# A decoder step on one core: the second half's stage input by four channel tiles, and feed-forward blocks of 6, 8 and 8 tiles

## Chip, cores and metric

One core of a Trainium2 chip runs the whole program. The metric is the device time of one execution in microseconds (us).

## The reference

A decoder trunk of four layers works on 512 prompt tokens and 64 sample tokens of width 1024. Each layer has a token mixer (gMLP, convolution, MLA, gMLP again) and a feed-forward, each followed by a residual layer norm, and each fed through a scale and shift computed from a condition (adaLN):

```python
for i in range(DEPTH):
    sh1p, sc1p, g1p, sh2p, sc2p, g2p = adaln(c_prompt, ada_w[i], ada_b[i])
    hp = xp * (1 + sc1p) + sh1p
    # op = mixer (i mod 3) of hp; the same for the samples with their own condition
    xp = layer_norm(ALPHA * xp + g1p * op, ln_mix_g[i], ln_mix_b[i])
    fp = swiglu_ffn(xp * (1 + sc2p) + sh2p, ffn_w_gate[i], ffn_w_up[i], ffn_w_down[i])
    xp = layer_norm(ALPHA * xp + g2p * fp, ln_ffn_g[i], ln_ffn_b[i])

def swiglu_ffn(h, wg, wu, wd):
    return (jax.nn.silu(h @ wg) * (h @ wu)) @ wd
```

The feed-forward is 2816 wide. The mixers, their caches and states are computed as well.

## The kernel before

**Layout.** The residual `xa` is kept transposed: 128 channels of each of `KT` = 8 channel tiles on the partitions, 576 tokens (512 of the prompt, then 64 of the samples) along the free axis. Tokens are worked in two halves `h` of `HALF` = 288; half 1 holds the last 224 prompt tokens (`HP`) and all samples.

**Products.** Each fp32 product is made of three fp32r matmuls, high x high, high x low, low x high (L736). The stage input is therefore the pair `h_hi`, `h_lo`, an inner activation the pair `a_hi`, `a_lo`, a weight the pair `w_hi`, `w_lo`. Weights come in units of up to 1024 words per partition through five slots: SyncE loads a unit into `w_raw` (L560) once the product that used the slot's former unit has ended (`plan.freed`, counted in `acc_ready`), GpSimd splits it (L669, L671), and TensorE takes it (`take_units`). The queue of units is laid down in order by `Plan`, and the `plan_` functions repeat the order of the products. Accumulators are four PSUM banks taken in turn (`acc_ready`, `acc_free`); four more banks serve statistics, transposes and adaLN.

**Feed-forward.** Its 22 inner tiles go in three blocks listed in `GU` (L372): gate and up products of a block (`gate_up`), then `down` of that block into all 8 output tiles, added to `xa` by VectorE. The last block's down product is `down_norm`, which also prepares the layer norm. Products that share a block's inner tiles run over as many k tiles as the block has. AdaLN matmuls of the next layer (`ada_pairs`) stand between: four behind the first half of the first two tiles, one behind every tile below 20 (`ada_behind`), one behind each of the first two `down`. For them SyncE puts loads of 1 MB between those of the units.

**Tail of a stage** (`down_norm`, on TensorE, VectorE and ScalarE). TensorE makes output tiles 0 to 3, both halves, then 4 to 7 of half 0, then matmuls against a matrix of ones that sum half 0 (mean and square) in the middle of tile 4 of half 1, then the rest of half 1. VectorE adds each product to `xa` (`add_norm`), reduces sums of tiles and of their squares (`sums` L1705, `squares` L1710), finishes the statistics (`Stats` L1723 to L1729), and normalises `xa` in steps of tiles 0-1, 2-3 and 4-7 (`normalise`, L1734 and L1736), each step counted in `n_ready`. For half 1 it does the same after the first half's input is out.

**Handover to the next stage.** ScalarE (`apply`, L1340) makes `hf` (fp32) and `h_hi` of four tiles at a time from normalised `xa`, two instructions a tile. VectorE then subtracts them into `h_lo` (`halves`, L1762) and counts `h_ready`, four times a stage: half 0 tiles 0-3, half 0 tiles 4-7, half 1 tiles 0-3, half 1 tiles 4-7. For half 1 VectorE first makes the samples' columns of `hf` with their own coefficients (`samples`, L1750), in one go for eight tiles. TensorE's `first_four` makes the first four products of half 0 by halves of k: k 0-3 of all four after the first count, k 4-7 after the second; the statistics of half 1 (`second_stats`) stand after the first of the four is done. These four are `first_halves` (gate and up of two tiles, or the convolution's) or `first_tokens` (two token tiles of two column blocks, for gMLP and MLA). Their results are taken off before half 1's `h_lo`: ScalarE and VectorE call `early()` (`ffn_first`, `conv_first`, `mla_first`, `gmlp_first`). The products of half 1 with the same weights then run one after the other, each over all of k.

The order of every engine is the order of this code; each engine waits for counted semaphores.

Of the kernel before, what the change touches and what calls it, by code (L numbers as in the profile page):

```python
# [97 lines left out]
def trunk(nc, A, O):  # L98
    ctx = ExitStack()
    with ctx:  # L100
# [271 lines left out]
        GU = ((0, 8), (8, 8), (16, 6))  # L372
# [351 lines left out]
        def _(pe):  # L724
# [49 lines left out]
            def product(out, ks, w_at, m_hi, m_lo, w_moves=False, waits=None):  # L774

                n = len(ks)
                for q, k in enumerate(ks):
                    if waits is not None and k % 4 == 0:
                        pe.wait_ge(h_ready, waits + k // 4)
# [90 lines left out]
            def first_halves(t, slots):  # L870

                def step(i, k, b):
                    s, c = slots[i], slice(k * P, (k + 1) * P)
                    for e, (w, a) in enumerate(((w_hi, h_hi), (w_hi, h_lo), (w_lo, h_hi))):
                        last = mm(pb[:, b, 0:HALF], w[:, s, c], a[:, k, 0:HALF], k == 0 and e == 0,
                                  k == KT - 1 and e == 2)
                    return last

                first_four(t, step, lambda _: slots.extend(take_units(2)))  # L880

            def first_tokens(t, slots, widths):

                def step(i, k, b):
                    blk, tt = divmod(i, 2)
                    n = widths[blk]
                    s, c = slots[blk][k // 4], slice(k % 4 * n, (k % 4 + 1) * n)
                    for e, (w, a) in enumerate(((w_hi, h_hi), (w_hi, h_lo), (w_lo, h_hi))):
                        last = mm(pb[:, b, 0:n], a[:, k, token_tile(tt)], w[:, s, c], k == 0 and e == 0,  # L890
                                  k == KT - 1 and e == 2)
                    return last

                def units(blk):
                    slots[blk] = take_units(2)

                first_four(t, step, units)
# [57 lines left out]
            def gate_up(first, count, wait_h, fresh, more):  # L955

                if fresh:
                    slots = []
                    first_halves(wait_h, slots)
                    ada_pairs(ADA_FIRST * more)  # L960
                    for s in slots:
                        half_product(s, KT, 1, (h_hi, h_lo), wait_h)
                for m in range(2 * fresh, count):
                    s_a, s_b = take_units(2)
                    for h in range(2):
                        for s in (s_a, s_b):
                            half_product(s, KT, h, (h_hi, h_lo))
                    ada_pairs(more * ada_behind(first + m))
# [15 lines left out]
            def gmlp(l):  # L984
# [3 lines left out]
                first_tokens(t, slots, (256, 256))  # L988
                for n, (gg, tt) in enumerate(first_order(GROUPS)):
                    if n < 4:  # L990
                        continue
                    if gg not in slots:
# [5 lines left out]
                            w_moves=True, waits=4 * t + 3 if n == 4 else None).then_inc(acc_ready, 1)  # L998
# [36 lines left out]
            def conv(l):  # L1035
# [9 lines left out]
                first_halves(t, slots)  # L1045
                for s in slots:
                    half_product(s, KT, 1, (h_hi, h_lo), t)
# [25 lines left out]
            def tok_major(chunk, tt, kts, hi, lo, waits=None):  # L1073
# [6 lines left out]
                        w_moves=True, waits=waits).then_inc(acc_ready, 1)  # L1080
                G.up()

            def mla(l):
                t = 2 * l
                slots = {}
                first_tokens(t, slots, (DCH[0][1], DCH[1][1]))
                for i, (c, tt) in enumerate(first_order(len(DCH))):
                    if i < 4:
# [3 lines left out]
                    tok_major((slots[c], lambda k: (k // 4, k % 4), DCH[c][1]), tt, KT, h_hi, h_lo,  # L1092
                              4 * t + 3 if i == 4 else None)
# [195 lines left out]
        def _(act):  # L1289
# [32 lines left out]
            def apply(t, early, loads=None):  # L1322

                for h in range(2):
# [5 lines left out]
                    for g in range(2):  # L1331
# [26 lines left out]
            def final():  # L1358
                t = 2 * DEPTH
                for h in range(2):  # L1360
                    deviation(t, h)
                    for m in range(KT):
                        if m in (0, 2, 4):
                            act.wait_ge(n_ready, 6 * t + 3 * h + m // 2 + 1)
# [212 lines left out]
        def _(dve):  # L1577
# [163 lines left out]
            def samples(t):  # L1741
# [3 lines left out]
                if t == 0:  # L1745
                    dve.wait_ge(h_ready, 2)
                o = hf[:, :, :, HP:].rearrange("p g i (b t) -> p (g i) b t", b=DEC_B)
                x = xa[:, :, SEQ:TOK].rearrange("p m (b t) -> p m b t", b=DEC_B)
                for src, coef, op in ((x, cs, ALU.mult), (o, cb, ALU.add)):
                    v.tensor_tensor(o, src, coef[:, t % RING_T, :, 1:NC].unsqueeze(3)  # L1750
                                    .to_broadcast([P, KT, DEC_B, DEC_T]), op)
# [13 lines left out]
            def down_norm(e, early=None, turn=False, by_half=False):  # L1765
# [525 lines left out]
            dve.drain().then_inc(n_ready, 6)  # L2291
            for g in range(2):
                halves(0, g)
            samples(0)
            for g in range(2):
                halves(1, g)
# [74 lines left out]
```

## Time and profile before

| | |
|---|---|
| time, median of 3 | 3607.05 us (3606.09 to 3609.25) |
| profiled execution | 3606.18 us, its span 3604.4 us |
| TensorE (PE) busy | 3241.4 us, 90% |
| VectorE (DVE) busy | 1775.0 us, 49% |
| GpSimd (POOL) busy | 1498.8 us, 42% |
| ScalarE (ACT) busy | 483.0 us, 13% |
| mean granted TensorE clock | 0.947 |

The page gives busy time by engine, then chains of work and costly groups. The timeline lists instructions with their start, duration in us, engine, line, operands, and in brackets the idle time before them with what ended it. A matmul's duration includes its way through the array, so two neighbours overlap; what counts is the distance of their starts. PEclk 1.00 is full clock, 0.50 half. SPq is SyncE's queue that issues loads.

### The profile page before, as it was taken

The page shows a single profiled execution, that of the slowest core. Times are in us where ns is not written, and L with a number is a line of the kernel's source. Part 1 is how long each engine was busy: PE and PEld are TensorE (multiplying, and loading weights), DVE is VectorE, ACT ScalarE, POOL GpSimd, SP SyncE. Part 2 cuts the span into 40 slices and gives each one's busy share as a digit, 9 for nine tenths or more (in the row PEclk, how much of TensorE's full clock was granted, in tenths as well). Part 3 has the DMA queues.
Part 4 walks back from the last instruction along what each step waited for, and adds up shares of the span by engine and source line. Part 5 has one row for each costly group of instructions (what it writes and reads, how often), then busy time and mean ns, then how long its engine had stood idle before and what let it go on. Part 6 is the DMA issues. An engine that isn't in the chain of part 4 may idle for free.

```text
span 3604.4 us, 54522 instructions
## 1 busy us (share of the span) xinstructions
PE 3241.4 (90%) x22732; PEld 2976.4 (83%) x22732; DVE 1775.0 (49%) x2754; ACT 483.0 (13%) x1004; POOL 1498.8 (42%) x876
## 2 busy tenths in 40 slices
PE   5979799999788699999778989999998988899996
PEld 4879789999766489999775548999988987899996
DVE  3174664433677764333654446434253456643436
ACT  2100030000210130000301202100013100210001
POOL 2343445454366445454320013455543343355551
PEclk8999999999899899999987989999998998999998
DMA  5532343442211143442212113534321232132221
GB/s 200 211 87 59 100 159 123 146 129 71 75 52 36 38 166 126 144 129 71 69 34 81 41 42 106 176 120 138 100 77 54 66 89 63 53 92 81 81 83 49
DMA packets 450515, 343.83 MB, mean 95 GB/s; under 512 B 24937, under 2 KB 435937, under 8 KB 437966
## 3 DMA queue, kind: packets, MB, share of 16 engines
q1 hardware_dynamic: 443104, 333.59, 29.3%
q10 hardware_dynamic: 7165, 6.76, 0.7%
q8 instruction: 180, 2.95, 0.3%
q14 instruction: 66, 0.53, 0.0%
HBM read 335.77 MB, written 5.25 MB: 95 GB/s over the span
## 4 chain that ended last, share of the span: by engine, by line
PE 74%; DVE 17%; issue 4%; DVEq 3%; ACT 1%; POOL 1%; POOLq 0%; DMA 0%; ACTq 0%; SPq 0%
PE pb L736 73%; DVE a_lo L1593 1%; DVE xa L1736 1%; DVE pb L2029 1%; DVE a_hi L1591 1%; DVE vn L1939 1%; DVE part L1710 1%; DVEq L1735 1%; DVE pb L1729 1%; DVE h_lo L1762 1%; DVE vn L1935 1%; DVE part L1705 1%; POOL w_lo L671 1%; PE pb L812 1%; DVE pgT L2229 1%
## 5 line engine op out<-in xcount | busy, mean ns | idle before, releaser
L669 POOL TENSOR_SCALAR w_hi<-w_raw 128x1024 fp32r<-128x1024 f32 (+2 forms) x416 | 449.9, 1082 | 1905.4 <-DMA w_raw<-in_ffn_w_up 437.8
L736 PE MATMUL pb<-h_hi,w_hi 128*128 128x288 f32 x3584 | 1084.3, 303 | 71.7 <-DVE h_lo L1762 50.8
L736 PE MATMUL pb<-h_lo,w_hi 128*128 128x288 f32 x3584 | 1071.3, 299 | 0.0
L736 PE MATMUL pb<-h_hi,w_lo 128*128 128x288 f32 x3584 | 1070.6, 299 | 0.0
L671 POOL TENSOR_TENSOR w_lo<-w_raw,w_hi 128x1024 fp32r<-128x1024 f32 (+2 forms) x416 | 964.5, 2319 | 62.4 <-issue 1.7
L736 PEld LDWEIGHTS pb<-h_hi,w_hi 128*128 128x128 f32 x3584 | 689.1, 192 | 123.2 <-issue 101.9
L736 PEld LDWEIGHTS pb<-h_lo,w_hi 128*128 128x128 f32 x3584 | 688.8, 192 | 0.3
L736 PEld LDWEIGHTS pb<-h_hi,w_lo 128*128 128x128 f32 x3584 | 687.8, 192 | 0.0
L736 PE MATMUL pb<-a_hi,w_hi 128*128 128x288 f32 x2176 | 648.3, 298 | 33.4 <-DVEq L2066 11.7
L736 PE MATMUL pb<-a_hi,w_lo 128*128 128x288 f32 x2176 | 642.5, 295 | 0.0
L736 PE MATMUL pb<-a_lo,w_hi 128*128 128x288 f32 x2176 | 642.2, 295 | 0.0
L736 PEld LDWEIGHTS pb<-a_hi,w_hi 128*128 128x128 f32 x2176 | 409.7, 188 | 43.7 <-issue 30.4
L736 PEld LDWEIGHTS pb<-a_lo,w_hi 128*128 128x128 f32 x2176 | 409.5, 188 | 0.9
L736 PEld LDWEIGHTS pb<-a_hi,w_lo 128*128 128x128 f32 x2176 | 409.6, 188 | 0.0
L1854 DVE TENSOR_TENSOR pr<-pb,sg 128x288 f32<-128x288 f32 x176 | 80.2, 458 | 623.5 <-PE pb L736 622.2
L1593 DVE TENSOR_TENSOR a_lo<-pr,a_hi 128x288 fp32r<-128x288 f32 x176 | 293.0, 1665 | 13.5 <-issue 0.4
L1374 ACT ACTIVATE sg<-pb 128x288 f32<-128x288 f32 x176 | 72.1, 411 | 1453.4 <-PE pb L736 1453.3
L736 PE MATMUL pb<-w_hi,h_hi 128*128 128x256 f32 (+1 forms) x760 | 222.1, 292 | 40.8 <-DVE h_lo L1762 37.0
L736 PE MATMUL pb<-w_hi,h_lo 128*128 128x256 f32 (+1 forms) x760 | 220.2, 290 | 0.0
L736 PE MATMUL pb<-w_lo,h_hi 128*128 128x256 f32 (+1 forms) x760 | 220.0, 289 | 0.0
L736 PEld LDWEIGHTS pb<-w_hi,h_hi 128*128 128x128 f32 x760 | 151.7, 200 | 47.5 <-issue 23.2
L1836 DVE SCALAR_TENSOR_TENSOR xa<-pb,gate,xa 128x288 f32<-128x288 f32 (+1 forms) x160 | 76.9, 481 | 155.2 <-PE pb L736 155.0
(274 smaller groups left out, 3276.3 us busy)
## 6 DMA issues: line engine op xcount, KB each, us to landing
ada_w<-in_ada_w SPq DMA_DIRECT2D x96, 1024.0 KB, 5.9
w_raw<-in_ffn_w_gate SPq DMA_DIRECT2D x88, 512.0 KB, 3.9
w_raw<-in_ffn_w_up SPq DMA_DIRECT2D x88, 512.0 KB, 3.6
w_raw<-in_gmlp_w_in SPq DMA_DIRECT2D x64, 512.0 KB, 5.4
w_raw<-in_ffn_w_down SPq DMA_DIRECT2D x64, 512.0 KB, 3.7
w_raw<-in_gmlp_w_out SPq DMA_DIRECT2D x32, 512.0 KB, 3.7
w_raw<-in_ffn_w_down SPq DMA_DIRECT2D x32, 384.0 KB, 3.2
w_raw<-in_conv_w_pw SPq DMA_DIRECT2D x24, 512.0 KB, 3.8
```

The source lines that it names most:

```text
L669: nc.gpsimd.tensor_scalar(w_hi[:, s, 0:w], w_raw[:, s, 0:w], 1.0, 1.0, ALU.mult, ALU.mult)
L671: nc.gpsimd.tensor_tensor(w_lo[:, s, 0:w], w_raw[:, s, 0:w], w_hi[:, s, 0:w].bitcast(F32), ALU.subtract).then_inc(split_full, 1)
L736: return nc.tensor.matmul(out, lhsT, rhs, start=start, stop=stop)
L812: last = nc.tensor.transpose(pb[0:cols, b, c0:c0 + rows], src, ident[0:rows, 0:rows])
L1374: fn(sg[:, q, :], pb[:, b, 0:HALF], func, **kw).then_inc(sg_ready, 1)
L1591: v.tensor_copy(hi, src)
L1593: return v.tensor_tensor(lo, src, hi.bitcast(F32), ALU.subtract)
L1705: v.reduce_sum(part[:, 0, n, half_cols(h)], xa[:, m0:m1, half_cols(h)].rearrange("p m t -> p t m"), AX.X)
L1710: v.reduce_sum(part[:, 1, n, half_cols(h)], sq[:, m0:m1, half_cols(h)].rearrange("p m t -> p t m"), AX.X)
L1729: v.reciprocal(self.rstd, self.rstd)
L1836: last_ = v.scalar_tensor_tensor(out=y, in0=ps[:, 0:w], scalar=gp, in1=y, op0=ALU.mult, op1=ALU.add)
L1854: v.tensor_tensor(pr[:, q, :], pb[:, (G.n + 1) % BANKS, 0:HALF], sg[:, q, :], ALU.mult).then_inc(acc_free, 2)
```

## The change

`GU` gets blocks of 6, 8, 8 tiles. `first_four`, `first_halves` and `first_tokens` get the half `h`, and half 1's first four products too are made k 0-3 of all four, then k 4-7; for `first_tokens` these are three further token tiles of block 0 and one of block 1. `normalise` is called for two tiles at a time (`n_ready` counts four times a half, eight a stage). In half 0 the first four tiles' `h_lo` stands between the steps 4-5 and 6-7. In half 1 VectorE works by four tiles: normalise, samples, (first time) `early()`, `h_lo`. `samples` takes a group `g`. The parameter `waits` of `product` and `tok_major` goes. The start of the kernel follows the same order.

```diff
-        GU = ((0, 8), (8, 8), (16, 6))
+        GU = ((0, 6), (6, 8), (14, 8))
...
-            def first_four(t, step, units):
+            def first_four(t, h, step, units=None):
...
                 for part_ in range(2):
-                    pe.wait_ge(h_ready, 4 * t + part_ + 1)
+                    pe.wait_ge(h_ready, 4 * t + 2 * h + part_ + 1)
                     for i in range(4):
                         if part_ == 0:
-                            if i % 2 == 0:
+                            if units is not None and i % 2 == 0:
                                 units(i // 2)
...
-                            if t and i == 0:
+                            if t and h == 0 and i == 0:
                                 second_stats()
...
-            def first_tokens(t, slots, widths):
+            def first_tokens(t, h, slots, widths):
                 def step(i, k, b):
-                    blk, tt = divmod(i, 2)
+                    blk, tt = ((0, 2), (0, 3), (0, 4), (1, 2))[i] if h else divmod(i, 2)
...
                 if fresh:
                     slots = []
-                    first_halves(wait_h, slots)
+                    first_halves(wait_h, 0, slots)
                     ada_pairs(ADA_FIRST * more)
-                    for s in slots:
-                        half_product(s, KT, 1, (h_hi, h_lo), wait_h)
+                    first_halves(wait_h, 1, slots)
...
-                            if m in (0, 2, 4):
-                                act.wait_ge(n_ready, 6 * t + 3 * h + m // 2 + 1)
+                            if m % 2 == 0:
+                                act.wait_ge(n_ready, 8 * t + 4 * h + m // 2 + 1)
...
-            def samples(t):
+            def samples(t, g):
                 dve.drain()
                 if t == 0:
-                    dve.wait_ge(h_ready, 2)
-                o = hf[:, :, :, HP:].rearrange("p g i (b t) -> p (g i) b t", b=DEC_B)
-                x = xa[:, :, SEQ:TOK].rearrange("p m (b t) -> p m b t", b=DEC_B)
+                    dve.wait_ge(h_ready, g + 1)
+                ms = slice(4 * g, 4 * g + 4)
+                o = hf[:, g, :, HP:].rearrange("p i (b t) -> p i b t", b=DEC_B)
+                x = xa[:, ms, SEQ:TOK].rearrange("p m (b t) -> p m b t", b=DEC_B)
...
                 first.normalise(2, 4)
                 add_norm(e, 4, 1)
-                first.normalise(4, KT)
-                if last:
-                    for m in range(5, KT):
-                        add_norm(e, m, 1)
-                else:
+                first.normalise(4, 6)
+                if not last:
                     halves(0, 0)
-                    for m in range(5, KT):
-                        add_norm(e, m, 1)
+                first.normalise(6, KT)
+                for m in range(5, KT):
+                    add_norm(e, m, 1)
...
-                for m0, m1 in ((0, 2), (2, 4), (4, KT)):
-                    second.normalise(m0, m1)
+                for g in range(2):
+                    for m0 in (4 * g, 4 * g + 2):
+                        second.normalise(m0, m0 + 2)
+                    if not last:
+                        samples(t, g)
+                        if g == 0:
+                            early()
+                        halves(1, g)
                 SQ.up(7)
-                if not last:
-                    early()
-                    samples(t)
-                    for g in range(2):
-                        halves(1, g)
```

The convolution, gMLP and MLA call the new forms in the same way (two calls of `first_halves` or `first_tokens`, the sequential list then starts at the ninth product instead of the fifth).

## Rows read from the trace of the kernel before

**Rows 1.** The page's busy times and shares, first line of its first part.

```profile
PE 3241.4 (90%) x22732; PEld 2976.4 (83%) x22732; DVE 1775.0 (49%) x2754; ACT 483.0 (13%) x1004; POOL 1498.8 (42%) x876
```

**Rows 2.** Waits of PE: total us, times, longest.

```profile
PE pb L736 <- DVE h_lo L1762: 87.7, 15, 10.2
...
PE pb L736 <- POOL w_lo L671: 3.8, 2, 3.5
```

**Rows 3.** Timeline, PE, gMLP to feed-forward: start, us, instruction, idle before.

```profile
480.40 0.40 PE L736 MATMUL pb<-h_hi,w_hi 128*128 128x288 f32 x1 [2.49 <-DVE h_lo L1762]
...
504.80 0.58 PE L736 MATMUL pb<-h_hi,w_hi 128*128 128x288 f32 x1 [5.68 <-DVE h_lo L1762]
```

**Rows 4.** Windows after that second wait: us, busy, PEclk, DMA share, GB/s.

```profile
505.20:509.20 4.00, 4.00 (x18) 4.00 (x18) 2.63 (x5) 0.00 (x0) 0.00 (x0) 0.50 0.00 0
...
510.00:514.00 4.00, 4.00 (x32) 4.00 (x32) 0.32 (x1) 0.41 (x1) 0.00 (x0) 1.00 0.60 193
```

**Rows 5.** Timeline, DVE, the same handover.

```profile
477.05 3.29 DVE L1762 TENSOR_TENSOR h_lo<-hf,h_hi 128x1152 fp32r<-128x1152 f32 x1
...
497.47 1.35 DVE L1734 TENSOR_TENSOR xa<-xa,pb 128x1152 f32<-128x1152 f32 x1
...
500.48 0.82 DVE L1854 TENSOR_TENSOR pr<-pb,sg 128x288 f32<-128x288 f32 x2 [0.23 <-issue]
...
501.39 0.69 DVE L1750 TENSOR_TENSOR hf<-xa,cs 128x512 f32<-128x512 f32 x1
...
503.30 1.36 DVE L1762 TENSOR_TENSOR h_lo<-hf,h_hi 128x1152 fp32r<-128x1152 f32 x1
```

**Rows 6.** Timeline, ACT, the same handover.

```profile
475.69 0.62 ACT L1340 ACTIVATE h_hi<-xa,cb,cs 128x288 fp32r<-128x288 f32 x1
...
496.15 0.57 ACT L1340 ACTIVATE hf<-xa,cb,cs 128x224 f32<-128x224 f32 x1 [1.68 <-DVE xa L1736]
...
499.42 0.56 ACT L1340 ACTIVATE h_hi<-xa,cb,cs 128x224 fp32r<-128x224 f32 x1
```

**Rows 7.** Timeline, tail with 8 k tiles (gMLP of layer 0).

```profile
450.05 2.27 DVE L1705 TENSOR_REDUCE part<-xa 128x288 f32<-128x1152 f32 x1
...
490.36 0.41 ACT L1318 ACTIVATE sqt<-pb 128x288 f32<-128x288 f32 x1 [6.14 <-PE pb L736]
```

**Rows 8.** Timeline, tail with 6 k tiles, before the convolution.

```profile
923.37 2.27 DVE L1705 TENSOR_REDUCE part<-xa 128x288 f32<-128x1152 f32 x1
...
936.86 1.33 PE L736 MATMUL pb<-part,ones 128*128 128x288 f32 x2 [2.91 <-DVEq L1711]
...
954.09 0.61 PE L736 MATMUL pb<-h_hi,w_hi 128*128 128x288 f32 x1 [5.24 <-DVE h_lo L1762]
...
966.49 0.41 ACT L1318 ACTIVATE sqt<-pb 128x288 f32<-128x288 f32 x1 [8.85 <-PE pb L736]
...
981.04 0.58 PE L736 MATMUL pb<-h_hi,w_hi 128*128 128x288 f32 x1 [9.37 <-DVE h_lo L1762]
```

**Rows 9.** Timeline, two other tails with 6 k tiles.

```profile
1732.95 2.28 DVE L1705 TENSOR_REDUCE part<-xa 128x288 f32<-128x1152 f32 x1
...
1772.74 0.41 ACT L1318 ACTIVATE sqt<-pb 128x288 f32<-128x288 f32 x1 [6.88 <-PE pb L736]
...
3546.03 2.27 DVE L1705 TENSOR_REDUCE part<-xa 128x288 f32<-128x1152 f32 x1
...
3580.19 0.41 ACT L1318 ACTIVATE sqt<-pb 128x288 f32<-128x288 f32 x1 [4.48 <-PE pb L736]
```

**Rows 10.** Timeline, SPq and POOL: refill of slots, split of unit 5.

```profile
510.42 0.38 SPq L560 DMA_DIRECT2D w_raw<-in_ffn_w_up  x1
...
513.62 0.38 SPq L560 DMA_DIRECT2D w_raw<-in_ffn_w_gate  x1
...
515.43 2.40 POOL L671 TENSOR_TENSOR w_lo<-w_raw,w_hi 128x1024 fp32r<-128x1024 f32 x1
```

**Rows 11.** Timeline, PE, last down product of layer 0.

```profile
904.89 0.40 PE L736 MATMUL pb<-a_hi,w_hi 128*128 128x288 f32 x1 [0.99 <-DVE a_lo L1593]
```

More of the change, by code:

```diff
@@ L772, in aux_bank, with product @@
                 return BANKS + X.n % BANKS
-            def product(out, ks, w_at, m_hi, m_lo, w_moves=False, waits=None):
+            def product(out, ks, w_at, m_hi, m_lo, w_moves=False):
                 n = len(ks)
                 for q, k in enumerate(ks):
-                    if waits is not None and k % 4 == 0:
-                        pe.wait_ge(h_ready, waits + k // 4)
                     s, cols = w_at(k)
@@ L875, in step @@
                     for e, (w, a) in enumerate(((w_hi, h_hi), (w_hi, h_lo), (w_lo, h_hi))):
-                        last = mm(pb[:, b, 0:HALF], w[:, s, c], a[:, k, 0:HALF], k == 0 and e == 0,
+                        last = mm(pb[:, b, 0:HALF], w[:, s, c], a[:, k, half_cols(h)], k == 0 and e == 0,
                                   k == KT - 1 and e == 2)
                     return last
-                first_four(t, step, lambda _: slots.extend(take_units(2)))
-            def first_tokens(t, slots, widths):
+                first_four(t, h, step, None if h else lambda _: slots.extend(take_units(2)))
+            def first_tokens(t, h, slots, widths):
                 def step(i, k, b):
-                    blk, tt = divmod(i, 2)
+                    blk, tt = ((0, 2), (0, 3), (0, 4), (1, 2))[i] if h else divmod(i, 2)
                     n = widths[blk]
@@ L895, in units @@
                     slots[blk] = take_units(2)
-                first_four(t, step, units)
+                first_four(t, h, step, None if h else units)
             def conv_stats(h):
@@ L987, in gmlp @@
                 slots = {}
-                first_tokens(t, slots, (256, 256))
+                for h in range(2):
+                    first_tokens(t, h, slots, (256, 256))
                 for n, (gg, tt) in enumerate(first_order(GROUPS)):
-                    if n < 4:
+                    if n < 8:
+                        if l == 0 and (gg, tt) == (0, TT - 1):
+                            ada_pairs(ADA_V[0])
                         continue
@@ L997, in gmlp @@
                             lambda k: h_hi[:, k, token_tile(tt)], lambda k: h_lo[:, k, token_tile(tt)],
-                            w_moves=True, waits=4 * t + 3 if n == 4 else None).then_inc(acc_ready, 1)
+                            w_moves=True).then_inc(acc_ready, 1)
                     G.up()
@@ L1044, in conv @@
                 slots = []
-                first_halves(t, slots)
-                for s in slots:
-                    half_product(s, KT, 1, (h_hi, h_lo), t)
+                for h in range(2):
+                    first_halves(t, h, slots)
                 state_turns()
@@ L1071, in conv, with tok_major @@
                 down_norm(KT, by_half=True)
-            def tok_major(chunk, tt, kts, hi, lo, waits=None):
+            def tok_major(chunk, tt, kts, hi, lo):
                 slots, slot_of, n = chunk
@@ L1079, in tok_major @@
                         lambda k: hi[:, k, token_tile(tt)], lambda k: lo[:, k, token_tile(tt)],
-                        w_moves=True, waits=waits).then_inc(acc_ready, 1)
+                        w_moves=True).then_inc(acc_ready, 1)
                 G.up()
@@ L1085, in mla @@
                 slots = {}
-                first_tokens(t, slots, (DCH[0][1], DCH[1][1]))
+                for h in range(2):
+                    first_tokens(t, h, slots, (DCH[0][1], DCH[1][1]))
                 for i, (c, tt) in enumerate(first_order(len(DCH))):
-                    if i < 4:
+                    if i < 8:
                         continue
@@ L1091, in mla @@
                         slots[c] = take_units(2)
-                    tok_major((slots[c], lambda k: (k // 4, k % 4), DCH[c][1]), tt, KT, h_hi, h_lo,
-                              4 * t + 3 if i == 4 else None)
+                    tok_major((slots[c], lambda k: (k // 4, k % 4), DCH[c][1]), tt, KT, h_hi, h_lo)
                 pe.wait_ge(mla_in, 64)
@@ L2290, in _ @@
             dve.drain().then_inc(coef_ready, 1)
-            dve.drain().then_inc(n_ready, 6)
+            dve.drain().then_inc(n_ready, 8)
             for g in range(2):
                 halves(0, g)
-            samples(0)
             for g in range(2):
+                samples(0, g)
                 halves(1, g)
```

10 lines of the change are left out of this document (5 added, 5 removed).

## The prediction

> **What bounds the kernel now.** I read the page's busy times first: TensorE is busy for 90% of the span [rows 1], so time can come only from what it waits for or from its clock. Next the list of waits, for TensorE alone: its costliest releaser by far is the subtraction that makes `h_lo`, 87.7 us in 15 waits [rows 2]; this is the wait for a stage's input, twice at each of the eight handovers, and it is what the change is about. Then one handover in order of time, gMLP to feed-forward in layer 0. TensorE waits 2.49 us before the first half's products and 5.68 us before the second half's [rows 3]. After a mixer (8 k tiles in its last product) TensorE idles little; after a feed-forward (6 k tiles) it idles 2.91 us for sums of VectorE, 5.24 us for the first half and 9.37 us for the second [rows 8]. VectorE's row of reductions sets that tail, not TensorE.
>
> **Part 1: blocks of 6, 8, 8.** The number of matmuls stays. The last block's down product goes from 6 to 8 k tiles: 16 half products get 2 k tiles x 3 matmuls more, 96 matmuls, and the first block's down loses the same 96. A product of 24 matmuls takes 3.20 us (the slots of two products in a row are refilled from 510.42 and 513.62, [rows 10]), so one matmul 0.133 us and 96 of them 12.8 us. Half of it (6.4 us) lies ahead of VectorE's first reduction of the tail and half behind it. So the first reduction comes 6.4 us earlier than now (12.8 removed ahead, 6.4 put back), and the other 6.4 us run while VectorE works through sums, root, normalising and `h_lo`, which don't depend on them. What is late next is that chain. I compare it in both forms, from the first reduction to the square behind the second half's mean: with 8 k tiles 450.05 to 490.36, 40.3 us [rows 7]; where TensorE may start at half rate I allow 0.5 more, 40.8. With 6 k tiles before the convolution 923.37 to 966.49, 43.1 us [rows 8]; before MLA 1732.95 to 1772.74, 39.8 us; at the very end, without a next stage, 3546.03 to 3580.19, 34.2 us [rows 9]. Gain before the convolution: 6.4 + (43.1 - 40.8) = 8.7. Before MLA: 6.4 - (40.3 - 39.8) = 5.9; before the second gMLP I take the same, 5.9. At the end TensorE's sums wait for the slower products, an estimate of 1 us: 6.4 - 1.0 = 5.4. Sum 25.9. Bounds: 6.4 nearly whole plus the cold start before the convolution four times, 32; if half of the moved work lands on the path after all (the 2.49 us of [rows 3] is all the slack that the 8-tile tail has left), 14.
>
> Also moved is the wait of a down product for the last gated tile, 0.99 us with 6 k tiles [rows 11]. Block 0 now has the short product, but in three of four layers adaLN matmuls stand ahead of it (an ada pair follows every tile below 20), the last block has 3.2 instead of 2.4 us of cover. Gain 0.8 x 2, say 1.5 (0 to 3). Loads and splits are the same ones in another order; the mixer tails run with 8-tile units, and TensorE waits for a split weight only twice in the whole span, 3.8 us in all [rows 2], so 0.
>
> **Part 2: the second half's input by four tiles.** Now VectorE normalises tiles 0-3, then 4-7 (two operations of 1.35 us, the first at 497.47), takes the first products off, makes all eight sample tiles (2 x 0.69), casts, and ends the first `h_lo` at 504.66 [rows 5]. With the change the operations of 4-7 and half the samples come behind it. New chain: tiles 0-3 normalised at 497.47; samples of half size 1.0 us (two of about 0.42 plus a drain each: 0.69 for 512 elements and 1.35 for 1152 give 0.16 fixed and 0.26 for 256); first products 0.9; ready at 499.4. But ScalarE makes `hf` and `h_hi` of these tiles only from 496.15 to 499.98 [rows 6], so that is what is late next: cast 0.37 and `h_lo` 1.36 end at 501.7, 2.95 us earlier.
>
> Against it stands the first half. There the normalising is split too, and `h_lo` of the first four waits for ScalarE (last of eight from 475.69, so 476.3, instead of 477.05) [rows 5, 6]: TensorE starts 0.7 us earlier, but VectorE idles those 0.66 us, pays the fixed part of the split operations (0.14, as drains overlap part of 2 x 0.16), and everything behind is 0.8 us later. TensorE started earlier and takes 0.3 us of that off its own statistics (an estimate), so 0.5 us is charged to each handover. Net 2.45 us earlier for the second half; for MLA and the second gMLP four copies make the first products about 0.5 us longer, so VectorE ends last, not ScalarE: what goes from ahead of its `h_lo` is 2.8 (tiles 4-7) and 0.6 (half the samples), 3.4 - 0.5 = 2.9. Bounds of part 2 per handover: 0 (if the ends are all ScalarE's) and 3.6, the whole of the removed operations.
>
> Next, the second `h_lo` pair. After the first: normalise 4-5 and 6-7 (3.0), ScalarE's last four (2.0), cast and `h_lo` (1.75), some 7.1 us after TensorE's start. TensorE has 48 matmuls, 6.4 us at full clock, 8.5 where 20 are at half rate. So a wait of 0.7 or none.
>
> **Where the feed-forward heads lose it again.** Unit 5 (tile 2's second weight) goes into the slot that the first product frees. Its load is issued at 510.42, the split ends at 517.83, 7.4 us later [rows 10]. Now this product is over 24 matmuls after the start, and all four end at 510.42 + 9.6 = 520.0, so the unit is 2.2 us early. With the change the first product ends only after 60 matmuls. Warm: start + 7.1 + 1.6 + 0.3 + 7.4 = start + 16.4, while the four end at start + 13.5: a new wait of 2.9 us. With a start at 502.35, tile 2 begins at 518.8 instead of 520.0: gain 1.2. Cold: 8.5 + 1.6 + 0.3 + 7.4 = 17.8, so 520.2: 0.2 lost. The same sum gives between +1 and -0.3 at the other three heads. I take 0 for the four together, less 1.4 for a clock that may fall in the new wait: the half-rate start at 504.80 cost 2.1 us (5.6 for the product instead of 3.2, of it 0.3 the end of the last matmul), four of them 8.4, of which I charge a sixth, since the 2.49 us wait left the clock up [rows 3]. On SyncE the unit stands ahead of three adaLN loads of 1 MB; those and units 6 and 7 move with it, and their slack of 2 us is used up but not passed.
>
> Before the convolution transposes stand between these products and the next unit: full gain, 2.5. Before MLA the unit is smaller: 2.9. Before gMLP slot 0 comes free after 84 instead of 72 matmuls of 256 columns (0.12 us by columns, an estimate): 84 x 0.12 + 7.4 = 17.5 against 144 x 0.12 = 17.3, so 2.7. First handover: TensorE is fed by the weights there, 0. End: the last step normalises two tiles instead of four ahead of ScalarE, 0.8 (two tiles of ScalarE's work, an estimate) less the splits, 0.5.
>
> **Sum.** 25.9 + 1.5 + 2.5 + 2.9 + 2.7 + 0.5 + 0 - 1.4 = 34.6, rounded to 34 for the small new instructions. The profiled execution took 3606.18 us with a span of 3604.4, 0.9 below the median of 3607.05; against the median 3573.
>
> **Rivals.**
> A. The heads get worse. For: the new wait of 2.9 us per feed-forward head is as long as waits after which matmuls ran at half rate; the 5.24 us and 9.37 us waits were followed by first matmuls of 0.61 and 0.58 us instead of 0.40 [rows 3, 8]. Four heads then lose 0.3 + 2.7 each, 12 us instead of 1.4: 3607 - 24 = 3583. Against: the 2.49 us wait left the clock up [rows 3].
> [...]
> B. Unit 5 is hidden and starts stay warm: the wait drops from 5.68 to 3.2 us, and the 2.1 us of cold matmuls go too. Three heads x (2.45 + 2.1), one x 2.45, some 16 us more: 3557. Against: 7.4 us from release to split is measured.
> C. The block order gives half, as the extra products delay the last sums (bound 14 above): 3585.
> D. Slower. One mechanism: the late weight unit. If the longer tail also holds back the slots of the next stage's first units, so that TensorE waits for units 1 to 3 at all seven handovers (the `w_lo` of one split alone takes 2.40 us [rows 10]), part 1 returns its 25.9, part 2 its 8, and each head adds a cold start of 2.1 us: 3607 + 4 x 2.1 - 1.5 = 3614, with part 1 and part 2 at 0. It decides once the wait for those units passes 5 us per handover; the mixer tails with 8 tiles show none of it [rows 2].
> E. The splitting isn't what I think (ScalarE sets all ends), part 2 gives 0: 3580, inside the range.
>
> **Chances.** Forecast (with E) 0.66, A 0.15, B 0.07, C 0.08, D 0.04. Range 3558 to 3588: it takes in the bounds of part 1, A and C. Some 0.2% (7 us) is what can be told from no change: faster 0.94, same 0.02 (the far end of C), slower 0.04 (D).
>
> **What would show it.** Right: TensorE's waits before the convolution, MLA and gMLP first halves near 2 us, with the wait on the sums gone; second-half waits near 3 us after gMLP and near 7 elsewhere; a new wait on GpSimd's `w_lo` of about 3 us at tile 2 of each feed-forward; waits on `h_lo` in all near 50 us. Wrong: first-half waits still near 5 us (then the tail is TensorE's), or no wait on `w_lo` (B), or half-rate matmuls at tile 2 (A).

## The result and the profile after

The changed kernel takes 3569.3 us (median of 4, 3562.1 to 3569.8), the kernel before beside it 3608.2 us (3606.1 to 3611.9): a ratio of 0.9895, 95% interval 0.9883 to 0.9907. Forecast were 3573 us, a range of 3558 to 3588, and faster. The profiled execution has a span of 3568.0 us, 36.4 us below that of before, and a mean granted clock of 0.952 (before 0.947).

The page's busy times of the changed kernel, to be held against [rows 1]:

```profile
PE 3238.6 (91%) x22732; PEld 2970.4 (83%) x22732; DVE 1794.8 (50%) x2802; ACT 484.0 (14%) x1004; POOL 1499.0 (42%) x876
```

TensorE has the same 22732 matmuls. Its busy time falls by only 2.8 us, so nearly all of the gain is idle time. VectorE has 48 instructions and 19.8 us more. Not all of that is new work: the 80 adds of the samples' part (`xa<-xa,smt`) take 64.7 us instead of 29.4, and 58.8 with the block order alone and 32.4 with the order alone. Waits of TensorE in the changed kernel (who was waited for, us in all, times, longest), to be held against [rows 2]:

```profile
PE pb L736 <- DVE h_lo L1762: 42.3, 13, 6.9
PE pb L736 <- POOL w_lo L671: 27.0, 15, 4.4
...
PE pb L736 <- DVEq L1710: 7.6, 9, 5.3
...
PE pb L736 <- DVE a_lo L1592: 6.3, 5, 1.4
```

The wait for the stage's input is halved, from 87.7 us, and the wait for split weights goes from 3.8 to 27.0 us. The third row is the wait for VectorE's partial sums; in the kernel before it was

```profile
PE pb L736 <- DVEq L1711: 21.2, 9, 7.8
```

TensorE's timeline from gMLP to feed-forward in layer 0 shows the second-half wait of 5.68 us [rows 3] now at 2.68, and a new one of 2.74 at tile 2:

```profile
482.93 0.40 PE L736 MATMUL pb<-h_hi,w_hi 128*128 128x288 f32 x1 [1.01 <-DVE xa L1698]
485.84 0.40 PE L736 MATMUL pb<-h_hi,w_hi 128*128 128x288 f32 x1 [1.07 <-POOL w_lo L671]
503.77 0.61 PE L736 MATMUL pb<-h_hi,w_hi 128*128 128x288 f32 x1 [2.68 <-DVE h_lo L1762]
521.06 0.61 PE L736 MATMUL pb<-h_hi,w_hi 128*128 128x288 f32 x1 [2.74 <-POOL w_lo L671]
```

At the handover to the convolution the first half's wait of 5.24 us [rows 8] is gone; two small ones stand in its place, and the second half waits 6.25 instead of 9.37 us:

```profile
950.07 0.40 PE L736 MATMUL pb<-h_hi,w_hi 128*128 128x288 f32 x1 [0.67 <-DVE xa L1698]
953.34 0.40 PE L736 MATMUL pb<-h_hi,w_hi 128*128 128x288 f32 x1 [1.43 <-POOL w_lo L671]
971.28 0.61 PE L736 MATMUL pb<-h_hi,w_hi 128*128 128x288 f32 x1 [6.25 <-DVE h_lo L1762]
```

To see where the time went I cut both spans at the first reduction of each tail, the instruction of [rows 7] at 450.05, in the changed kernel at 452.20 (first reductions and squares of the mean, VectorE and ScalarE, changed kernel; they answer to [rows 7] and [rows 8]):

```profile
452.20 2.27 DVE L1704 TENSOR_REDUCE part<-xa 128x288 f32<-128x1152 f32 x1
...
492.33 0.41 ACT L1317 ACTIVATE sqt<-pb 128x288 f32<-128x288 f32 x1 [6.64 <-PE pb L736]
...
919.57 2.27 DVE L1704 TENSOR_REDUCE part<-xa 128x288 f32<-128x1152 f32 x1
...
959.84 0.41 ACT L1317 ACTIVATE sqt<-pb 128x288 f32<-128x288 f32 x1 [6.66 <-PE pb L736]
```

| stretch between first reductions | before, us | after, us | difference |
|---|---|---|---|
| start to tail 1 | 450.1 | 452.2 | +2.1 |
| the four with a feed-forward (1, 3, 5, 7) | 473.3, 473.5, 473.1, 450.6 | 467.4, 467.5, 463.5, 445.1 | -27.1 |
| the three with a mixer (2, 4, 6) | 336.1, 467.2, 422.2 | 333.3, 464.0, 415.5 | -12.7 |
| last tail to the end | 58.4 | 59.6 | +1.2 |

### The profile page after: what moved, and what is told of

It is laid out like the page before. It is cut to its first block, busy times and chain, and to the rows that moved or that the text cites. A ratio compares the mean times of both kernels' runs of the same rounds, so it can differ in the third digit from the quotient of the medians.

```text
span 3568.0 us, 54595 instructions
## 1 busy us (share of the span) xinstructions
PE 3238.6 (91%) x22732; PEld 2970.4 (83%) x22732; DVE 1794.8 (50%) x2802; ACT 484.0 (14%) x1004; POOL 1499.0 (42%) x876
## 3 DMA queue, kind: packets, MB, share of 16 engines
q8 instruction: 180, 2.95, 0.3%
## 4 chain that ended last, share of the span: by engine, by line
issue 45%; POOL 22%; PE 16%; POOLq 10%; DVE 4%; SPq 2%; DVEq 1%; ACT 0%; DMA 0%; ACTq 0%
POOL w_lo L671 22%; PE pb L736 16%; POOLq L670 10%; DVE pb L2028 1%; SPq L634 1%; SPq L636 1%; SPq L638 1%; DVE a_lo L1592 0%; DVE xa L1735 0%; DVE full L2012 0%; DVE yc L2036 0%; PE pb L810 0%; DVE yc L2033 0%; DMA out_y_prompt<-yo 0%; DVE qaT L2163 0%
## 5 line engine op out<-in xcount | busy, mean ns | idle before, releaser
L669 POOL TENSOR_SCALAR w_hi<-w_raw 128x1024 fp32r<-128x1024 f32 (+2 forms) x416 | 442.4, 1064 | 1869.0 <-DMA w_raw<-in_ffn_w_up 424.8
L736 PE MATMUL pb<-a_hi,w_hi 128*128 128x288 f32 x2176 | 649.7, 299 | 30.6 <-DVEq L2065 11.3
L1592 DVE TENSOR_TENSOR a_lo<-pr,a_hi 128x288 fp32r<-128x288 f32 x176 | 278.7, 1584 | 13.5 <-issue 0.4
L736 PEld LDWEIGHTS pb<-w_hi,h_lo 128*128 128x128 f32 x760 | 149.7, 197 | 0.1
```

The lines of the kernel that those rows point to most:

```text
L669: nc.gpsimd.tensor_scalar(w_hi[:, s, 0:w], w_raw[:, s, 0:w], 1.0, 1.0, ALU.mult, ALU.mult)
L736: return nc.tensor.matmul(out, lhsT, rhs, start=start, stop=stop)
L1592: return v.tensor_tensor(lo, src, hi.bitcast(F32), ALU.subtract)
```

## The experiments

The theory that went to the chip: the block order is worth some 25 us, through VectorE's chain in the tail; the input by four tiles is worth some 9, with its gain at the feed-forward heads eaten by the late weight unit of tile 2. Rivals: the late unit costs more than that (clock), or nothing; TensorE sets the tail. Each ratio below is to the kernel before on the same chip, with its 95% interval.

**The changed kernel again**, for the span's own scatter, at two later times.

> The changed kernel as it stands, once more beside the others on one chip. Expected 3569 us, 38 below the kernel before. The first reduction of the first tail came 2.15 us later in the changed kernel's profile (452.2 against 450.05). If that belongs to the change it stands at 452 again; if it is chance of the start-up it moves by some microseconds.

> The changed kernel for that comparison: 38 us below the kernel before, as before.

Measured: 3563.9 us, 0.9896 (0.9883 to 0.9909), span 3560.4; and 3562.2 us, 0.9882 (0.9864 to 0.99). The first reduction of tail 1 stands at 449.96 us in the one and at 452.05 in the other. Over all profiles it stands at 450.05 and 450.09 with the old blocks, and with other blocks at 449.96 once and at 450.4 to 454.0 in the ten others. Whether the 2.1 us are chance or come with the block order stays open.

**The block order alone.** The kernel before with one line changed:

```diff
-        GU = ((0, 8), (8, 8), (16, 6))
+        GU = ((0, 6), (6, 8), (14, 8))
```

> The kernel before with blocks of 6, 8, 8 and nothing else. Theory (the tails behind a feed-forward are set by VectorE's reductions, so 6.4 us of products per tail become free): 26 to 28 us below the kernel before, 3581; the four intervals from a feed-forward's first reduction to the next stage's second-half input stay within 1 us of the 8-tile mixer tails; second-half waits of TensorE stay at 5.7 us (three) and 9 to 10 us (four). Rival (the extra products land on the path): 14 us, 3594.

> Blocks of 6, 8, 8 alone, a second profile. The first came from the fastest of six executions (3572.15; the others 3576 to 3590). Theory: the executions differ by where matmuls ran at half rate and by when GpSimd's split of units 2 and 3 ended (it waited 3.3 us at the convolution's head in the first profile); then this profile shows a lower clock, or more wait on w_lo, by the time that it is longer. Rival: it differs in VectorE's chain.

Measured: 3584.1 us (3572.2 to 3590.1), 0.9945 (0.9933 to 0.9957), that is 20 to 21 us, where 26 to 28 were expected. The second profile is of an execution of 3585.5 us, its span 13.4 us longer than the first one's: 10.1 of them in the mixer stretches, at a mean clock of 0.948 instead of 0.951, with the same waits on `w_lo` (11.8 and 11.7 us). The lower clock fits the expectation, the splits as the cause don't. TensorE's wait for the sums is 7.6 us in 9, as in the whole change. Two heads show what the order of half 0 has to do with it. TensorE, then VectorE and GpSimd, before the convolution with the block order alone:

```profile
947.48 0.40 PE L736 MATMUL pb<-h_hi,w_hi 128*128 128x288 f32 x1 [0.55 <-DVE h_lo L1762]
954.18 0.61 PE L736 MATMUL pb<-h_hi,w_hi 128*128 128x288 f32 x1 [3.27 <-POOL w_lo L671]
```

```profile
946.07 1.36 DVE L1762 TENSOR_TENSOR h_lo<-hf,h_hi 128x1152 fp32r<-128x1152 f32 x1
...
946.12 3.57 POOL L671 TENSOR_TENSOR w_lo<-w_raw,w_hi 128x1024 fp32r<-128x1024 f32 x1
950.86 3.27 POOL L671 TENSOR_TENSOR w_lo<-w_raw,w_hi 128x1024 fp32r<-128x1024 f32 x1
```

The input is there early, but the second passes (`w_lo`) of two splits take 3.57 and 3.27 us instead of the 2.40 of [rows 10], TensorE waits 3.27 us for one of them and goes on with the 0.61 us matmul of the half rate. The square of the second mean follows the first reduction by 43.1 us here and 43.7 before MLA, against 40.3 and 40.0 in the whole change: about 3 us at each of two heads.

**The order alone.** The changed kernel with the old blocks:

```diff
-        GU = ((0, 6), (6, 8), (14, 8))
+        GU = ((0, 8), (8, 8), (16, 6))
```

> The changed kernel with blocks of 8, 8, 6 as before. Theory: the second halves start 3 us earlier relative to their tail, the four feed-forward heads give it back in a wait of 2.7 us for the weight unit of tile 2, so only convolution, MLA and gMLP heads keep 2 to 3 us each: 7 to 11 us below the kernel before, 3598. Rival (the two parts need one another): sum of both parts differs from the whole by over 4 us.

Measured: 3595.4 us (3591.5 to 3601.4, 11 runs), 0.9973 (0.9965 to 0.9982): 10 us. The stretches with a feed-forward measure 473.7, 474.1, 471.8 and 452.0 us, as before the change (sum +1.1), those with a mixer 332.1, 463.7 and 416.0 (sum -13.7). So this part brings nothing where a feed-forward head follows the tail, and its gain lies at the other heads, as forecast. Its wait for sums is 20.7 us in 10: the blocks alone take that one away.

**The second half's first products one after the other**, all else as changed. This is meant to free the first slot early and so hide tile 2's late unit:

```diff
             def first_four(t, h, step, units=None):
+                if h:
+                    for i in range(4):
+                        pe.wait_ge(acc_free, G.n + i + 1)
+                        for part_ in range(2):
+                            if i == 0:
+                                pe.wait_ge(h_ready, 4 * t + 2 + part_ + 1)
+                            for k in range(4 * part_, 4 * part_ + 4):
+                                last = step(i, k, (G.n + i) % BANKS)
+                        last.then_inc(acc_ready, 1)
+                    G.up(4)
+                    return
```

> The changed kernel, but the second half's four first products run one after the other over all of k, as before; VectorE's new order stays. Theory: the first product now stops after 12 matmuls for tiles 4-7 (ready 7.1 us after the start), so all four end 18.3 us after the start instead of 14 (convolution, MLA, gMLP) or of tile 2's start at 17.3 (feed-forward, where the late unit hides the rest): 1 us at four heads, 4 at the convolution, 2.5 at two others, 14 us slower than the changed kernel, so nearly all of what the new order gave. Rival (VectorE's order alone is what counts): under 4 us.

Measured: 3593.3 us (3587.2 to 3595.5), 0.9961 (0.9947 to 0.9976), by the ratios 23 to 28 us slower than the changed kernel, not 14. TensorE, feed-forward head of layer 0:

```profile
503.05 0.37 PE L736 MATMUL pb<-h_hi,w_hi 128*128 128x288 f32 x1 [2.77 <-DVE h_lo L1773]
510.13 0.61 PE L736 MATMUL pb<-h_hi,w_hi 128*128 128x288 f32 x1 [4.93 <-DVE h_lo L1773]
```

It starts as early, runs out of input after 12 matmuls, waits 4.93 us for tiles 4-7 and goes on at half rate (a granted clock of 0.50 from 510.5 to 514.5, 18 matmuls; in the kernel before 33 matmuls in the same 4 us). At the seven heads this second wait comes to 30.4 us (3.86 to 5.08). The input by four tiles is thus worth nothing without the products by halves of k, and it costs: the kernel with the same products and half 1's input in one go (below) takes 3581.6 us.

**Blocks of 7, 8, 7**, all else as changed:

```diff
-        GU = ((0, 6), (6, 8), (14, 8))
+        GU = ((0, 7), (7, 8), (15, 7))
```

> The changed kernel with blocks of 7, 8, 7. Theory (VectorE sets the tail; every tile moved into the last block frees 3.2 us a tail): half of the gain of the blocks, 10 to 13 us slower than the changed kernel. Rival (what counts is that the last block is full, as its products outlast VectorE's reductions): nearer to the whole loss, 20 us or more, or nearer to none.

Measured: 3582.5 us (3576.4 to 3586.2), 0.9936 (0.9922 to 0.995), 14 to 19 us slower than the changed kernel: between the 10 to 13 expected of half the gain and the 20 or more of the rival, that the last block has to be full. Half of what the blocks bring by themselves would be 10, half of the forecast 13. The wait for the sums lies between the two, 13.0 us in 9:

```profile
PE pb L736 <- DVEq L1710: 13.0, 9, 6.5
```

So the gain of the order grows with the length of the last block's product. The few us beyond half can't be told from scatter, so the rival isn't ruled out by the time; the wait between the two speaks for the first reading.

**The first half's second step as before.** In half 0, tiles 4-7 are normalised ahead of the first four tiles' `h_lo`, all else as changed:

```diff
                 first.normalise(4, 6)
+                first.normalise(6, KT)
                 if not last:
                     halves(0, 0)
-                first.normalise(6, KT)
```

> The changed kernel, but in half 0 the first four tiles' h_lo stands behind both normalise steps 4-5 and 6-7, as before. Theory (VectorE idles 0.66 us for ScalarE there, and all behind is late by it, while TensorE's earlier start only meets a wait for a bank and a weight unit, 0.7 and 1.4 us): from first reduction to second-half mean 0.6 us shorter at seven handovers, 4 us faster than the changed kernel. Rival (the earlier start of TensorE is worth its price): no change or 1 to 3 us slower.

Measured: 3572.9 us (3569.1 to 3578.9), 0.9913 (0.9898 to 0.9927): some 6 to 11 us slower than the changed kernel, not 4 faster. From first reduction to square the seven tails take 286.9 us together, against 281.7 to 282.0 in three profiles of the changed kernel: 5 us longer, not 4 shorter. The cause is in the durations of one instruction. VectorE's first `h_lo` of the handover and the split beside it on GpSimd, in this kernel:

```profile
481.33 3.00 DVE L1762 TENSOR_TENSOR h_lo<-hf,h_hi 128x1152 fp32r<-128x1152 f32 x1
...
480.75 2.36 POOL L671 TENSOR_TENSOR w_lo<-w_raw,w_hi 128x1024 fp32r<-128x1024 f32 x1
```

and in the changed kernel:

```profile
478.47 1.54 DVE L1762 TENSOR_TENSOR h_lo<-hf,h_hi 128x1152 fp32r<-128x1152 f32 x1 [0.62 <-ACT h_hi L1339]
...
478.95 3.30 POOL L671 TENSOR_TENSOR w_lo<-w_raw,w_hi 128x1024 fp32r<-128x1024 f32 x1
```

The same subtraction takes 1.36 us with GpSimd idle. Here it started while a split was running and ended 1.2 us after that split's end (483.11 to 484.33); in the changed kernel it comes ahead of this pass, and the pass is the one that takes longer (from `h_lo`'s end at 480.01 to 482.25 is 2.24 us, near the 2.36 of a split by itself). Whichever starts second waits for the other. Over the seven heads:

| first, second `h_lo` of half 0, mean us | first | second | both, sum of 7 heads |
|---|---|---|---|
| before | 3.16 | 2.12 | 37.0 |
| blocks alone | 2.89 | 2.02 | 34.3 |
| changed (two later profiles: 30.7, 30.9) | 1.68 | 2.68 | 30.5 |
| this kernel | 3.06 | 2.10 | 36.2 |

5.6 us of VectorE's chain come back with the old place of the step, about the size of the loss. What decides is the place. In this kernel `h_lo` starts 27.3 us after the first reduction, 0.2 to 0.8 us behind the start of a `w_lo` pass; in the changed kernel it starts at 26.3, in spite of its wait of 0.6 us for ScalarE, and 0.5 to 0.9 us ahead of that pass. There it meets only the rest of the split's first pass (`w_hi`, L669), and ends about 1.2 us after that one's end, which gives the 1.54 to 1.91 us. In the kernel before it starts at 27.0 (26.4 to 27.5), 0.3 to 0.7 us behind the pass:

```profile
476.77 2.36 POOL L671 TENSOR_TENSOR w_lo<-w_raw,w_hi 128x1024 fp32r<-128x1024 f32 x1
```

**Blocks and half 0 as changed, half 1 in one go**: the kernel of the products one after the other, with half 1 of the tail nearly as before (the first products' results ahead of all samples, both `h_lo` last; the normalising and the samples keep their new, smaller steps).

```diff
-                for g in range(2):
-                    for m0 in (4 * g, 4 * g + 2):
-                        second.normalise(m0, m0 + 2)
-                    if not last:
-                        samples(t, g)
-                        if g == 0:
-                            early()
-                        halves(1, g)
+                for m0 in range(0, KT, 2):
+                    second.normalise(m0, m0 + 2)
+                if not last:
+                    early()
+                    for g in range(2):
+                        samples(t, g)
+                    for g in range(2):
+                        halves(1, g)
                 SQ.up(7)
```

> Blocks of 6, 8, 8 and the first half's new order (h_lo of tiles 0-3 between the normalise steps), with the second half as before: all eight tiles normalised, first products, all samples, then both h_lo, and whole products. Theory formed from the last runs (the first half's order saves the 2.5 us wait and the half-rate starts behind it; it was worth 6 us): 5 to 7 us below blocks alone, 3578, second-half waits again 5.7 and 9 to 10 us. Rival (it is worth nothing without the second half's order, whose starts it makes warm): the same as blocks alone, 3584.

Measured: 3581.6 us (3577.6 to 3587.8), 0.9936 (0.9922 to 0.9951): 2 to 3 us below the block order alone, inside the intervals, where 5 to 7 were expected. The traces show two parts of it. From first reduction to square the seven tails take 282.0 us, with blocks alone 291.2 and 294.0: 9 to 12 us less, of which the `h_lo` of half 0 has 3.5 (30.9 against 34.3). From the square to the second half's first `h_lo` they take 97.6 us, with blocks alone 91.6: the smaller steps of half 1 give 6 us back. So the first half's order saves more than the total shows. The other 15 to 19 us up to the changed kernel are half 1, its order and its products by halves of k together.

**AdaLN matmuls moved into the new wait.** In the feed-forward head two of the four pairs go behind the second half's first products, where TensorE waits for tile 2's unit:

```diff
-                    ada_pairs(ADA_FIRST * more)
+                    ada_pairs(2 * more)
                     first_halves(wait_h, 1, slots)
+                    ada_pairs(2 * more)
```

> The changed kernel with two of the four adaLN pairs of each feed-forward head moved behind the second half's first products. Theory of the late weight unit: the second half starts at the same time, as it waits for VectorE (TensorE's wait there goes from 2.7 to 4.5 us), and the wait of 2.7 us at tile 2 falls to 0.9 in the three layers that have these pairs: 5 us faster than the changed kernel, 3564. Rival (the longer wait lets the clock fall, 2.1 us each): the gain is gone or 1 us is lost. Rival two (the wait at tile 2 is not for that unit): no change of that wait.

> The changed kernel with two adaLN pairs of each feed-forward head behind the second half's first products, once more beside the changed kernel, since the first comparison lay within the intervals. Theory: 3 to 5 us faster than the changed kernel. Rival: nothing.

Measured: 3560.5 us, 0.9876 (0.9862 to 0.989), and again 3563.6 us, 0.9881 (0.9863 to 0.9899), beside 3563.9 and 3562.2 of the changed kernel: no difference that lasts. TensorE, first of the two profiles:

```profile
503.30 0.61 PE L736 MATMUL pb<-h_hi,w_hi 128*128 128x288 f32 x1 [4.39 <-DVE h_lo L1763]
...
517.64 1.92 PE L736 MATMUL pb<-ada_w,cact 128*32 128x512 f32 x16
...
520.40 0.40 PE L736 MATMUL pb<-h_hi,w_hi 128*128 128x288 f32 x1 [0.84 <-POOL w_lo L671]
```

The wait at tile 2 falls from 2.74 to 0.84 us as expected, yet tile 2 starts 17.1 us after the second half instead of 17.3, and 17.4 and 18.0 at the next two feed-forward heads instead of 17.3 and 16.5: its start is set by the unit, not by what TensorE does meanwhile. And the moved pairs are missing in the wait ahead, 4.39 us instead of 2.68. The two waits sum to 5.2 instead of 5.4 us. My expectation counted a wait that is filled as time gained; the work that fills it came from another wait.

## Why the prediction was right, and where its terms were off

**Part 1, 25.9 us forecast.** The mechanism is shown: the wait on the sums falls by 13.6 us (21.2 to 7.6), only the block order takes it away, and with the half-way blocks it lies between. By itself the block order gives 20 to 21 us, 5 below the forecast. At two heads the stretch from reduction to square is 6.5 us longer than in the whole change (there `h_lo` comes first and delays the splits); I had set the gain before the convolution at 8.7 with the half-rate start gone, and with blocks alone a half-rate start stays, behind the wait for the unit. In the whole change it is gone: the time from first reduction to square is 40.1 to 40.5 us at all seven heads, where I allowed 40.3 and 40.8.

**The last gated tile, 1.5 us forecast.** The sum is right, the place wrong. The waits fall from 8.4 to 6.3 us in all, but the last block's own wait, which I had at about 0.2 with 3.2 us of cover, rose from 0.99 [rows 11] to 1.36:

```profile
895.53 0.40 PE L736 MATMUL pb<-a_hi,w_hi 128*128 128x288 f32 x1 [1.36 <-DVE a_lo L1592]
```

**Part 2, 2.95 us earlier to the second half's `h_lo`, less 0.5.** The first term is right, the second is not. From the square of the second half's mean to the start of its first `h_lo` it took 12.9 to 13.4 us, now 10.0: 2.9 to 3.4 less. VectorE at the head of layer 0, to be held against [rows 5]:

```profile
499.62 0.43 DVE L1750 TENSOR_TENSOR hf<-xa,cs 128x256 f32<-128x256 f32 x1
500.12 0.42 DVE L1750 TENSOR_TENSOR hf<-hf,cb 128x256 f32<-128x256 f32 x1
...
501.99 0.29 DVE L1760 CAST h_hi<-hf 128x256 fp32r<-128x256 f32 x1 [0.45 <-ACT h_hi L1339]
502.36 1.36 DVE L1762 TENSOR_TENSOR h_lo<-hf,h_hi 128x1152 fp32r<-128x1152 f32 x1
...
509.54 1.36 DVE L1762 TENSOR_TENSOR h_lo<-hf,h_hi 128x1152 fp32r<-128x1152 f32 x1
```

The samples' two instructions take the 0.42 us each that I had worked out; ScalarE ends the chain ahead of the cast, as said; the second pair ends at 510.9, 7.1 us after TensorE's start, as said. The 0.5 us charged to each of seven handovers (3.5 in all) for VectorE's idling in half 0 did not show as a loss: with the order alone the seven stretches from reduction to square take 281.2 us, before 287.5, so there is a gain of 6.3. The `h_lo` of half 0 got 0.92 us shorter per head (6.4 in all), which pays for it. This term had the wrong sign; that the total still fits is partly luck. I had the 3.29 us of that instruction in [rows 5] beside 1.36 of the same form, and did not ask why.
On this the Trainium skill (SBUF — State Buffer, "🔬 SBUF: two separate sides") says that a VectorE operation with two inputs in SBUF and a GpSimd operation that reads SBUF lock a shared pair of ports, and that the one that starts second blocks for the whole of the other. The rows agree: second starts end 1.2 us (for 1.36) and 2.24 us (for 2.36) after the first one's end.

**The feed-forward heads, 0 and -1.4 us.** The new wait is there at all four, 2.74, 2.70, 2.66 and 2.81 us for the 2.9 worked out. SyncE's issue and GpSimd's split of this unit, to be held against [rows 10]:

```profile
513.56 0.38 SPq L560 DMA_DIRECT2D w_raw<-in_ffn_w_up  x1
...
517.47 1.05 POOL L669 TENSOR_SCALAR w_hi<-w_raw 128x1024 fp32r<-128x1024 f32 x1 [26.24 <-DMA w_raw<-in_ffn_w_up]
518.66 2.35 POOL L671 TENSOR_TENSOR w_lo<-w_raw,w_hi 128x1024 fp32r<-128x1024 f32 x1
```

From issue to the split's end it is 7.45 us (7.4 worked out). The half-rate matmuls of rival A come too, here from the new wait on, and after the second half's wait as before (windows: us, busy by engine, granted clock, DMA share, GB/s; before [rows 4]):

```profile
504.20:506.20 2.00, 2.00 (x10) 2.00 (x10) 1.85 (x4) 0.90 (x2) 0.00 (x0) 0.50 0.00 0
...
521.50:523.50 2.00, 2.00 (x10) 2.00 (x10) 0.21 (x1) 2.00 (x5) 0.00 (x0) 0.50 0.99 418
```

Tile 2 starts 68.9, 69.0, 68.1 and 69.2 us after the first reduction (before 69.8, 70.3, 70.7 and 69.7; at layer 0 that is 519.83, not the 520.0 of my sum). That is 5.2 us earlier over the four heads, but it doesn't last. ScalarE's `sg` that follows the third product of tile 2, before and after at layer 0:

```profile
529.61 0.41 ACT L1374 ACTIVATE sg<-pb 128x288 f32<-128x288 f32 x1 [3.71 <-PE pb L736]
...
532.36 0.41 ACT L1373 ACTIVATE sg<-pb 128x288 f32<-128x288 f32 x1 [5.95 <-PE pb L736]
```

It stands 79.6, 80.0, 80.5 and 79.5 us after the first reduction before, and 80.2, 80.5, 78.0 and 80.4 after: 0.5 us earlier in sum (0.4 later and 0.1 earlier in the two later profiles). From tile 2's start to this point it took 9.8 us at each head before, now 11.3, 11.4, 9.9 and 11.2. Of the four new waits three were followed by half rate, for 11 to 16 matmuls, one by none, and the head without it is the one that keeps its gain. So rival A's condition held at three heads, at 1.4 to 1.7 us each instead of 3. The forecast of 0 less 1.4 for the clock is right in sum: with the order alone the four feed-forward stretches are 1.1 us longer than before. The single terms were larger than I had them, an earlier start of 5.2 us and a half rate that costs 4.7.

**The other waits.** On `h_lo` 42.3 us in all (near 50 forecast), 2.68 after three of the mixers, 6.25 after the last, where no adaLN matmuls stand between, and 6.25 to 6.68 elsewhere. What I had not forecast is in the 27.0 us on `w_lo`: beside 10.9 at tile 2 there are 10.0 at the seven first halves (1.07 to 1.59 each). TensorE now starts there earlier than the third or fourth unit is split. That is rival D's mechanism, at 1.4 us a head instead of the 5 from which it would have decided.

**The end, 0.5 us of gain and 1.0 of loss forecast.** From the first reduction to the square 35.4 us instead of 34.2 [rows 9]: the loss, as said. TensorE's wait for the sums is shorter, 5.28 us instead of 7.79, but ends 34.1 us after the first reduction instead of 32.8:

```profile
3542.50 2.29 PE L736 MATMUL pb<-part,ones 128*128 128x288 f32 x4 [5.28 <-DVEq L1710]
```

The gain of 0.5 isn't there: from the square to the end it is 24.1 us, before 24.2.

**Sum.** Feed-forward stretches -27.1 (forecast -25.7 for the terms in them), mixer stretches -12.7 (-9.4), end +1.2 (+0.5), start +2.1 (0; open, as said): -36.4 against -34.6. The misses are within 4 us each and fall both ways; the time came nearer than the terms. Open: blocks alone and order alone give 21 and 10 us, together 31, the whole change 38 to 43. So the two parts need one another, as the rival of the run with the order alone had it. At the two heads above the order takes 2.8 and 3.7 us off the stretch from reduction to square with the new blocks, and 1.2 and 1.0 with the old ones: 4 of the 7 to 12. The rest is as large as the intervals.

## What to carry to other kernels

Moving work from ahead of another engine's serial chain to beside it (here the longer product into the last block) was worth 20 to 21 of the 25.6 us moved, and costs one line; look for it first where the chain's own sums are what the matmul engine waits for. An input handed over in smaller pieces paid here only once its consumer could work on one piece for about as long as the next took. A wait filled with work from another wait gained nothing here, as something else set its end, and an instruction that takes twice its usual time in the trace is a question to answer before its step is moved.

## What the runs showed of the hardware

- One kernel's executions differ by up to 18 us (blocks alone, 3572.2 to 3590.1), with a clock of 0.951 in a profile of 3570.3 us and 0.948 in one of 3583.7. The stretches of the convolution and of MLA measured 333.3, 333.2 and 328.6, and 464.0, 459.6 and 464.9 us in profiles of kernels that don't differ there. A single profile can't settle a difference under 5 us in such a stretch.
